# Recurrent steps of a delta rule with joint stationary operands, and its inverse's products by 64-blocks on two quadrants of the array

## What is computed

```python
def unit_lower_inverse(lmat):            # 64 x 64 per chunk and head
    inv = eye + nil                      # nil = -lmat
    for _ in range(log2(C) - 1):         # five rounds for C = 64
        powk = powk @ powk
        inv = inv @ (eye + powk)
    return inv

# chunk_gated_delta_rule(q, k, v, g, beta), T = 256, C = 64, so 4 chunks
u = tinv @ (v * beta)
w = tinv @ (k * beta * exp(gc))
a_intra = (q @ k.T) * decay
def step(S, xs):                         # S: 128 x 128 per head
    v_new = u_n - w_n @ S
    o_n = q_n @ S + a_n @ v_new
    S = S * c_n + k_n.T @ v_new
    return S, o_n                        # scan over the 4 chunks
```

## Time and profile before

| what | value |
|---|---|
| time, median of 3 runs | 2325.9 us (2325.8 to 2326.24) |
| the profiled execution | 2326.02 us, span of its trace 2324.2 us |
| TensorE matmul busy (PE) | 2305.2 us, 99% |
| TensorE weight loads busy (PEld) | 2041.7 us, 88% |
| VectorE busy (DVE) | 1617.7 us, 70% |
| ScalarE busy (ACT) | 1073.8 us, 46% |
| GpSimd busy (POOL) | 39.5 us, 2% |
| granted TensorE clock | 1.00 |
| mean memory traffic | 172 GB/s |

### The profile page before, as it was taken

The page is one execution under the profiler, slowest core; times in us unless marked ns, Lnnn a source line. Parts: engine busy times, 40 slices in busy tenths (PEclk is TensorE's granted clock), DMA queues, the critical chain, the costliest instruction groups (busy, mean ns, idle before and its releaser), DMA issues.

```text
span 2324.2 us, 37134 instructions
## 1 busy us (share of the span) xinstructions
PE 2305.2 (99%) x13964; PEld 2041.7 (88%) x13964; DVE 1617.7 (70%) x2287; ACT 1073.8 (46%) x1398; POOL 39.5 (2%) x55
## 2 busy tenths in 40 slices
PE   9999999999999999999999999999999999999998
PEld 9999988888888888888899999888888888888887
DVE  5876665877787778555568676658778787785455
ACT  5454434644444444444455444346444444444443
POOL 0000010000000000000000000100000000000000
PEclk9999999999999999999999999999999999999999
DMA  7533326555665556555544433275655565555553
GB/s 243 170 121 109 124 94 204 177 180 183 196 195 185 180 187 215 194 182 203 199 146 146 137 102 124 74 235 168 193 181 180 193 195 190 180 201 207 188 185 141
DMA packets 295368, 401.29 MB, mean 173 GB/s; under 512 B 9320, under 2 KB 269570, under 8 KB 283522
## 3 DMA queue, kind: packets, MB, share of 16 engines
q1 hardware_dynamic: 294996, 400.19, 52.2%
q10 hardware_dynamic: 302, 0.12, 0.0%
HBM read 398.20 MB, written 2.10 MB: 172 GB/s over the span
## 4 chain that ended last, share of the span: by engine, by line
PE 94%; DVE 3%; DVEq 1%; ACT 1%; issue 1%; DMA 0%; ACTq 0%; SPq 0%; POOLq 0%; POOL 0%
PE ps L1528 28%; PE ps L1509 15%; PE ps L1510 15%; PE ps L1511 15%; PE ps L1534 14%; PE ps L673 2%; PE ps L678 1%; PE ps L730 1%; DVE w_lo L1159 1%; PE ps L743 1%; DVEq L1387 0%; ACT w_hi L942 0%; PE ps L736 0%; PE ps L1657 0%; DMA raw<-in_w_in 0%
## 5 line engine op out<-in xcount | busy, mean ns | idle before, releaser
L942 ACT ACTIVATE w_hi<-raw 128x1024 fp32r<-128x1024 f32 x740 | 779.7, 1059 | 984.1 <-PE ps L1534 522.1
L1159 DVE TENSOR_TENSOR w_lo<-raw,w_hi 128x1024 fp32r<-128x1024 f32 x744 | 895.8, 1224 | 465.4 <-ACT w_hi L942 457.5
L1528 PE MATMUL ps<-h_both,w_hi 128*128 128x512 f32 x2816 | 885.3, 396 | 1.2 <-DVE h_both L1181 1.2
L1534 PEld LDWEIGHTS ps<-h_both,w_lo 128*128 128x128 f32 x2816 | 529.0, 188 | 124.7
L1534 PE MATMUL ps<-h_both,w_lo 128*128 128x256 f32 x2816 | 553.9, 278 | 0.0
L1528 PEld LDWEIGHTS ps<-h_both,w_hi 128*128 128x128 f32 x2816 | 428.9, 189 | 1.9 <-issue 1.6
L1509 PE MATMUL ps<-w_hi,h_both 128*128 128x512 f32 x960 | 376.1, 392 | 0.9 <-DVE w_lo L1159 0.9
L1511 PE MATMUL ps<-w_hi,h_both 128*128 128x512 f32 x960 | 373.7, 389 | 0.0
L1510 PE MATMUL ps<-w_lo,h_both 128*128 128x512 f32 x960 | 373.7, 389 | 0.0
L1509 PE MATMUL ps<-h_both,w_hi 128*128 128x256 f32 x1216 | 354.7, 292 | 2.1 <-DVE h_both L1181 2.1
L1510 PE MATMUL ps<-h_both,w_hi 128*128 128x256 f32 x1216 | 343.8, 283 | 0.0
(11 more groups left out here) (201 smaller groups left out, 1251.6 us busy)
## 6 DMA issues: line engine op xcount, KB each, us to landing
raw<-in_ffn_w_up SPq DMA_DIRECT2D x88, 2048.0 KB, 8.0
raw<-in_ffn_w_down SPq DMA_DIRECT2D x44, 2048.0 KB, 7.7
raw<-in_w_in SPq DMA_DIRECT2D x37, 2048.0 KB, 8.2
raw<-in_w_out SPq DMA_DIRECT2D x64, 512.0 KB, 6.4
x<-in_x SPq DMA_DIRECT2D x4, 512.0 KB, 7.0
raw<-in_w_in SPq DMA_DIRECT2D x4, 512.0 KB, 8.6
scratch<-in_norm_mix_post SPq DMA_DIRECT2D x2, 1024.0 KB, 9.5
scratch<-in_norm_ffn_post SPq DMA_DIRECT2D x2, 1024.0 KB, 10.0
```

What stands on the lines that cost most here:

```text
L942: act.activation(w_hi[:, own(q, s), :], raw_part(l, q, s), ACT.Copy).then_inc(hi_done, 1)
L1159: dve.tensor_tensor(w_lo[:, own(q, s), :], raw_part(l, q, s), w_hi[:, own(q, s), :].bitcast(F32), ALU.subtract).then_inc(lo_done, 1)
L1528: pe.matmul(ps[:, up_bank(q - P_UP, i), :], w_hi[:, own(q, s), c:c + P], h_both[:, k, :, :].rearrange("p a n -> p (a n)"), start=k == 0, s ...
L1534: return pe.matmul(ps[:, up_bank(q - P_UP, i), 0:T], w_lo[:, own(q, s), c:c + P], h_hi[:, k, :], start=False, stop=True, skip_group_check= ...
```

## The change

Three edits, all in the delta stage.

1. **State steps.** `w` and the decayed `q` of a chunk are stored side by side (`wq`, in the order w0, q0, q1, w1), and one 128x128 stationary operand does the work of L730 and L736 for a head. The result is written to all 128 partitions: `w @ S` on the chunk's own 64, `q @ S` on the other 64. For chunk 0 it goes to bank 6, for chunk 1 to bank 2. TensorE waits for the state of each head apart, and the state products of the two heads go to banks 3 and 7, each with its own signal. The fill is issued in quarters (`quarter_a`, `out_quarter`): one quarter between `wq @ S` and the wait for `v_new`, one at the end of each of the first three steps, and 2.5 halves instead of 2 after the last. On VectorE, in the two groups of the loop, `taps(2, ...)` goes to n = 0 (tap 1 ahead of the state update, tap 2 behind it) and n = 1 (tap 3), and `more(11)` goes from n = 0 to n = 3.
2. **The inverse.** The ten products of the five rounds are issued as eight 64x64 matmuls each instead of four 128x128, alternating between the quadrant of chunk 0 and that of chunk 1, each chunk in a bank of its own (3 and 2, 6 and 5). ScalarE's copy and VectorE's update are issued per chunk. The waits in front of the products are `hold`.
3. **The outputs.** o is now in two banks by chunk, so ScalarE squares and copies by halves of 64 partitions, the final product with the gate is two instructions, and TensorE waits for `o_copied` before it turns the next group's q, k and v. The pooling products move to banks 3 and 6.

```diff
-                 states=(1, 1, 1, 1), out=2, end=0)
+                 states=(0.5, 0.5, 0.5, 0.5), steps=(0.5, 0.5, 0.5), out=2.5, end=0)
...
+        wq = scr[:, 5:7, :].rearrange("p a (m n) -> p (a m) n", m=2).rearrange("p m (c n) -> p m c n", c=4)
+        w_of, qd_of = wq[:, :, 0:4:3, :], wq[:, :, 1:3, :]
+        RESID_BANKS, STEP_BANKS = (3, 2), (6, 5)
+        def chunk(ap, c):
+            return mats(ap)[CH * c:CH * (c + 1), :, CH * c:CH * (c + 1)]
+        def state_bank(c):
+            return 2 if c else 6
...
                 act.wait_ge(sem("residual"), 5 * v - 4 + k)
-                act.activation(resid, ps[:, 3, :], ACT.Copy).then_inc(sem("resid_copied"), 1)
+                for c in range(2):
+                    act.activation(chunk(resid, c), chunk(ps[:, RESID_BANKS[c], :], c),
+                                   ACT.Copy).then_inc(sem("resid_copied"), 1)
...
-            act.wait_ge(sem("o_done"), v)
-            act.activation(e2, ps[:, 6, :], ACT.Square).then_inc(sem("o_squared"), 1)
-            act.activation(o_m, ps[:, 6, :], ACT.Copy).then_inc(sem("o_copied"), 1)
+            for c in range(2):
+                act.wait_ge(sem("o_done"), 2 * v - 1 + c)
+                r = slice(CH * (1 - c), CH * (2 - c))
+                act.activation(e2[r, :], ps[r, state_bank(c), :], ACT.Square).then_inc(sem("o_squared"), 1)
+                act.activation(o_m[r, :], ps[r, state_bank(c), :], ACT.Copy).then_inc(sem("o_copied"), 1)
...
                 dve.wait_ge(sem("inv_product"), 5 * v - 4 + k)
-                dve.scalar_tensor_tensor(inv, inv, 2.0, ps[:, 6, :], ALU.mult,
-                                         ALU.subtract).then_inc(sem("inv_ready"), 1)
+                for c in range(2):
+                    dve.scalar_tensor_tensor(chunk(inv, c), chunk(inv, c), 2.0, chunk(ps[:, STEP_BANKS[c], :], c),
+                                             ALU.mult, ALU.subtract).then_inc(sem("inv_ready"), 1)
+                dve.drain()
...
-                if n == 0:
+                if last and n == 0:
                     more(11)
-                if n == 1:
-                    taps(2, (1, 2))
-                if n == 2:
-                    taps(2, (3,))
+                if not last and n < 2:
+                    taps(2, (1 + 2 * n,))
+                if not last and n == 3:
+                    more(11)
                 if n < 3:
-                    dve.wait_ge(sem("state_add"), 3 * v - 2 + n)
                     for h in range(2):
+                        dve.wait_ge(sem("state_add"), 6 * v - 5 + 2 * n + h)
                         sh = state[:, h * P:(h + 1) * P]
                         dve.scalar_tensor_tensor(sh, sh, gate_g[:, 5 + c, 2 * h + t:2 * h + t + 1],
-                                                 ps[:, 3, h * P:(h + 1) * P], ALU.mult, ALU.add)
-                    dve.drain().then_inc(sem("state_ready"), 1)
+                                                 ps[:, 3 + 4 * h, 0:P], ALU.mult,
+                                                 ALU.add).then_inc(sem("state_ready"), 1)
+                    dve.drain()
+                    if not last and n == 0:
+                        taps(2, (2,))
...
+            def chunks(banks, w, r):
+                for m in range(4):
+                    for c in range(2):
+                        ins = pe.matmul(chunk(ps[:, banks[c], :], c)[:, m, :], chunk(w, c)[:, m, :], chunk(r, c)[:, m, :],
+                                        start=m == 0, stop=True, skip_group_check=True)
                 return ins
...
             for k in range(5):
-                pe.wait_ge(sem("inv_ready"), 6 * v - 5 + k)
-                four(3, inv, low_m).then_inc(sem("residual"), 1)
+                hold(pe, sem("inv_ready"), 12 * v - 10 + 2 * k)
+                chunks(RESID_BANKS, inv, low_m).then_inc(sem("residual"), 1)
                 more(fill["residual"][k])
-                pe.wait_ge(sem("resid_copied"), 5 * v - 4 + k)
-                four(6, resid, inv).then_inc(sem("inv_product"), 1)
+                hold(pe, sem("resid_copied"), 10 * v - 8 + 2 * k)
+                chunks(STEP_BANKS, resid, inv).then_inc(sem("inv_product"), 1)
                 more(fill["step"][k])
...
             for n in range(4):
                 t, c = n // 2, n % 2
                 r = slice(CH * c, CH * (c + 1))
-                pe.wait_ge(sem("state_ready"), 4 * v - 3 + n)
                 for h in range(2):
                     m = 2 * h + t
-                    cols = slice(m * P + CH * c, m * P + CH * (c + 1))
-                    ins = pe.matmul(ps[r, 2, h * P:(h + 1) * P], w_t[:, cols], state[:, h * P:(h + 1) * P],
-                                    start=True, stop=True)
+                    pe.wait_ge(sem("state_ready"), 8 * v - 7 + 2 * n + h)
+                    ins = pe.matmul(ps[:, state_bank(c), m * P:(m + 1) * P],
+                                    wq[:, m, 2 * c:2 * c + 2, :].rearrange("p c n -> p (c n)"),
+                                    state[:, h * P:(h + 1) * P], start=h == 0, stop=False, skip_group_check=True)
                 ins.then_inc(sem("ws_done"), 1)
-                for h in range(2):
-                    m = 2 * h + t
-                    cols = slice(m * P + CH * c, m * P + CH * (c + 1))
-                    pe.matmul(ps[r, 6, m * P:(m + 1) * P], qd_t[:, cols], state[:, h * P:(h + 1) * P],
-                              start=h == 0, stop=False, skip_group_check=True)
                 more(fill["states"][n])
...
+                if n < 3:
+                    more(fill["steps"][n])
             more(fill["out"])
+            pe.wait_ge(sem("o_copied"), 2 * v)
```

More of the change, by code:

```diff
@@ L98 @@
 FILL_FULL = dict(turned=8, normed=2, products=2, n_turned=1, residual=(1, 1, 1, 1, 1), step=(1, 1, 1, 1, 2), uw=2,
-                 states=(1, 1, 1, 1), out=2, end=0)
+                 states=(0.5, 0.5, 0.5, 0.5), steps=(0.5, 0.5, 0.5), out=2.5, end=0)
 FILL_LAST = dict(turned=7, normed=2, products=2, n_turned=1, residual=(1, 1, 1, 1, 1), step=(1, 1, 1, 1, 1), uw=2,
-                 states=(1, 1, 1, 1), out=2, end=2)
+                 states=(0.5, 0.5, 0.5, 0.5), steps=(0.5, 0.5, 0.5), out=2.5, end=2)
 FEW_LATER = {0: 0, 1: 1, 3: 2, 4: 3, 5: 4, 7: 5, 8: 6, 9: 7, 10: 8, 11: 9, 12: 10, 14: 11, 15: 12}
@@ L491, in swa_dve, with delta_dve @@
             finish(1)
-        def delta_dve(dve, l, g, more, finish, taps, windowed=lambda: None, second=3):
+        def delta_dve(dve, l, g, more, finish, taps, windowed=None, second=3):
             v = l * NG + g + 1
+            last = windowed is not None
             dve.drain()
@@ L742, in delta_pe @@
                         m = 2 * h + t
-                        ins = pe.matmul(ps[:, 3, h * P:(h + 1) * P], kdec[r, m * P:(m + 1) * P],
-                                        v_new[r, h * P:(h + 1) * P], start=True, stop=True)
-                    ins.then_inc(sem("state_add"), 1)
+                        pe.matmul(ps[:, 3 + 4 * h, 0:P], kdec[r, m * P:(m + 1) * P], v_new[r, h * P:(h + 1) * P],
+                                  start=True, stop=True).then_inc(sem("state_add"), 1)
                 for h in range(2):
@@ L748, in delta_pe @@
                     cols = slice(m * P + CH * c, m * P + CH * (c + 1))
-                    ins = pe.matmul(ps[r, 6, m * P:(m + 1) * P], attn[r, cols], v_new[r, h * P:(h + 1) * P],
-                                    start=False, stop=True, skip_group_check=True)
-                if n == 3:
+                    ins = pe.matmul(ps[CH * (1 - c):CH * (2 - c), state_bank(c), m * P:(m + 1) * P], attn[r, cols],
+                                    v_new[r, h * P:(h + 1) * P], start=False, stop=True, skip_group_check=True)
+                if n >= 2:
                     ins.then_inc(sem("o_done"), 1)
+                if n < 3:
+                    more(fill["steps"][n])
             more(fill["out"])
+            pe.wait_ge(sem("o_copied"), 2 * v)
             if tail is None:
@@ L1520, in part_a @@
                 if q < P_UP:
-                    for half in range(2):
-                        half_a(l, q, j, n, s, half)
+                    for kk in range(4):
+                        quarter_a(l, q, j, n, s, kk)
                 else:
@@ L1555, in both_tiles, with quarter_a @@
                 return ins
-            def half_a(l, q, j, n, s, half):
-                if half == 0:
+            def quarter_a(l, q, j, n, s, kk):
+                if kk == 0:
                     if s == 0:
@@ L1562, in half_a @@
                     pe.wait_ge(lo_done, l * SUBS + 8 * j + (4 * q + s + 9))
-                for kk in (2 * half, 2 * half + 1):
-                    ins = both_tiles(q, s, kk)
-                if half == 1:
+                ins = both_tiles(q, s, kk)
+                if kk == 3:
                     ins.then_inc(sub_used, 1)
@@ L1702, in out_half @@
                     pe.wait_ge(lo_done, l * SUBS + (4 * q + s + 9))
-                for t in range(TT):
```

(13 more changed lines are left out.)

58 lines of the change are left out of this document (33 added, 25 removed).

## The result

The changed kernel takes 2309.61 us (median of four, 2309.45 to 2309.81) beside 2326.07 us for the kernel before in the same comparison: a ratio of 0.9929, interval 0.9912 to 0.9946. The profiled execution has a span of 2307.6 us instead of 2324.2, 16.6 less. The forecast was 2306 us (its sum gives 2305.8): the time lies inside the forecast's range, 3.6 us above the forecast.

What follows compares the result with a forecast made beforehand. TensorE, busy 99% of the span, was taken to bound the kernel. 2326.0 - 18.6 (steps) + 3.9 (given back) - 7.2 (products) + 1.7 (round k = 1) = 2305.8, forecast 2306 us, range 2300 to 2332.

Steps and rivals of the forecast that it cites:

- the rest at nothing: Squares and copies by halves, the `o_copied` wait and SP's transfers: claimed to cost nothing.
- The product, 0.77: Each of the inverse's 60 products takes 0.77 us instead of 0.89, quadrants overlapping: -7.2 us.
- The choice between overlap and turns: Inverse products: quadrants overlapping saves 7.2 us, taking turns costs 19.2 us; the forecast took overlap.
- The steps, 3.30: State steps of the delta stage take 3.30 us instead of 4.09, 3.1 us saved per group: -18.6 us.
- What the steps give back, 3.9: Waits from finer state steps: 0.8 us over all steps plus 3.1 in four loop groups, +3.9 us.
- The 0.8 us that I spread over all steps: State steps: 0.04 us of waiting per step because less fill covers `v_new`, 0.8 us in all.
- Round k = 1, 1.7: Inverse round where taps hold VectorE: product about 0.4 us later in four groups, +1.7 us.
- the quadrants take turns (2329): Rival for the inverse: no overlap, a product takes 1.21 us, total 2329 us; chance 0.20.
- each move costs a load (2353): Rival for the inverse: each quadrant move adds 0.05 us, product 1.61, total 2353 us; chance 0.08.
- "Partly" (2317): Rival for the inverse: matmuls overlap but loads don't, or order hinders; product about 0.99, total 2317 us; chance 0.14.
- the steps give back twice as much (2310): Rival for the state steps: VectorE late in more steps, 8 us given back, total 2310 us; chance 0.08.

Runs made afterwards that it cites:

- e4_vector_order: Changed kernel, VectorE order in the loop groups' steps moved: `more(10)` behind `v_new` at n = 0, each tap behind the state update; 2305.58 us.
- e11_before_spread: Kernel before the change, with the first convolution's three taps spread over inverse rounds k = 1, 2 and 3 in the loop groups; 2324.31 us.
- e9_tail: Changed kernel with VectorE reordered in steps and inverse (taps spread over rounds), plus the last group's low part 11 made one place earlier; 2301.75 us.
- e3_by_chunk: Changed kernel, each inverse product issuing all four blocks of chunk 0, then those of chunk 1, instead of alternating; 2321.29 us.

## Why the prediction came out 3.6 us low

The forecast had the right mechanism at each of its three places, and missed a fourth. Two terms were wrong by much, the size of a product and "the rest at nothing", and both to the same side.

- **The product, 0.77.** Measured 0.80: eight pairs at 0.058 are 0.46 where 0.44 was forecast, and the visit costs 0.34 for 0.33. The term was 60 x 0.12 = 7.2 and is 60 x 0.09 = 5.4, or by the unrounded distances (0.802) 1.9 us less than forecast: **+1.9 us**. The choice between overlap and turns, on which 26 us hung, was right. By the Trainium skill ("TensorEngine Tiling (Array Packing)", Key Properties), that different tiles load and multiply in parallel, the trace agrees: 7 ns between the two quadrants' passes. By the Trainium skill's rule of some 62 ns per matmul where microcode decodes ("TensorE: Matmul & The Clock Gate", Part 2: What happens when you issue a matmul) sixteen starts would, by my estimate from that page, span 15 x 0.062 = 0.93 us; the trace has 0.46, and 7 ns between neighbours, so the rule doesn't bind here.
- **The steps, 3.30.** Right: 3.28, and 3.24 to 3.27 in the last groups. The 18.6 us stand. The joint pass at 0.11, `kdec` and `attn` as before, all as forecast.
- **What the steps give back, 3.9.** The two places were named rightly (state behind tap 1, `v_new` behind tap 2), with 0.75 us per loop group. They cost 0.26 and 0.57, and a third was missed: `more(10)`, which the change leaves ahead of the first `v_new`, where a quarter of fill no longer covers it. I had looked at what the change moves, and not at what it leaves in a place that has become narrower. Measured 4 x 1.05 = 4.2 by the rows. The 0.8 us that I spread over all steps isn't there except for some 0.05 in the last groups. Together **+0.4 us**; `e4_vector_order` takes 4.0 of it away. That the term came out so near is luck: the missed place (4 x 0.22) stands in for the 0.8 that isn't there.
- **Round k = 1, 1.7.** Measured 1.5: **-0.2 us**. VectorE's pair of chunk updates was put at 0.15 more than one (0.86 for 0.69: 0.17), ScalarE's two copies at up to 0.3 more (0.78 for 0.60: 0.18). `e11_before_spread` fits the 4 x 0.43 = 1.7 us that stood in the kernel before.
- **"The rest at nothing".** This is the step that failed. The last group of each layer has its low parts made by VectorE just in time, and in the changed kernel fill reaches them sooner. The view of waits of the kernel before already had two such waits of 0.9 us in all, a place without slack that I didn't price. They are 2.3 us now by that view; by the distances between starts, where the uncovered load counts too, the change added 0.5 us per layer inside the inverse (ten products should save 0.87 and the stretch is 0.35 and 0.38 shorter) and 0.41 behind the output's transposes: **+1.8 us** in two layers. `e9_tail` confirms the second of these by taking 0.75 away; the first is read from the trace and no run takes it away.

Sum: 1.9 + 0.4 - 0.2 + 1.8 = 3.9 us, against 3.6 between forecast and result. The 0.3 is about what the lateness in the steps was read too large: the three readings make 1.05 us per loop group, and counted by fill `e4_vector_order` takes 0.96 away, 3.9 in all, which is the forecast's own figure. Counted by fill against the kernel before, the change saves 0.47 to 0.55 us in the inverse and 2.14 in the steps of a loop group, and 0.35 to 0.38 and 3.10 in the last group, which then loses 0.40 behind the output's transposes: 16.7 us over both layers, for the 16.6 by which the span is shorter.

The rivals: that the quadrants take turns (2329) and that each move costs a load (2353) are refuted by the 7 ns between their passes and by a product of 0.80 us. "Partly" (2317) is what `e3_by_chunk` shows of a kernel that groups its passes by chunk, at 1.08 us per product and not 0.99. That the steps give back twice as much (2310) comes as near to the number (2309.6) as one can ask, and not to the reason: the steps gave back 4.2, not 8.

**What stays open.** The waits inside the last group's inverse were read but not tried. How many passes TensorE looks ahead was read from `e3_by_chunk`'s distances at this one size. Whether each chunk needs its own bank wasn't tried, so the part that the second bank plays is unknown. Why the first fill matmul starts up to 0.5 us earlier or later from trace to trace was not looked into.

## What to carry to other kernels

When a change shortens TensorE's work between two hand-overs, list every item that VectorE and ScalarE have queued ahead of the next hand-over, those that the diff doesn't touch included, and those places first where the engine waits already. Here reordering VectorE's queue brought another 7.3 us on top of the change's 16.5, and the finer split changed from a loss of 1.8 to a gain of 0.7. Independent products on different quadrants should be issued alternately, not one after the other (here 2309.61 us for 2321.29). And before a difference of half a microsecond is explained, see where in the two traces it arises: here 0.37 us arose before the edited code ran.
